# A two-block transformer kernel: the output product of the attention block in three split passes, its parts split between the heads, the pooling three heads earlier, the shift put into the rows by products

## The reference, cut to what matters

```
xl  = xl + g1 * (concat[a, b, p, h] @ w_out)      # a: differential attention, b: neighbourhood attention,
                                                  # p: pooling, h: long convolution; 256 features each
hl2 = rmsnorm(xl, norm2_g) * (1 + sc2) + sh2
gates = top-2 of softmax(hl2 @ router_w), inside the best group of 4 experts
for e in 16 experts:  out += gates[:, e] * ((silu(hl2 @ w1[e]) * (hl2 @ w3[e])) @ w2[e])
```

## Time and profile before

| | us |
|---|---|
| median of three runs | 1447.33 |
| the runs | 1447.38, 1447.33, 1444.16 |
| the profiled execution, device time | 1444.78 |
| its span, first to last instruction | 1442.9 |
| TensorE busy in the span | 1291.6 (90%) |
| DVE, ACT, POOL busy | 839.9, 569.7, 146.6 |
| mean granted TensorE clock | 0.936 of full speed |

### The profile page before, as it was taken

One profiled execution on the slowest core, in us unless ns is written; L12 is line 12 of the kernel. 1 busy time (PEld: TensorE's weight loads), 2 busy tenths in 40 slices (PEclk: granted clock), 3 DMA queues, 4 the chain that ended last, 5 costly groups with the idle time before them and its releaser, 6 DMA issues.

```text
span 1442.9 us, 16957 instructions
## 1 busy us (share of the span) xinstructions
PE 1291.6 (90%) x6470; PEld 929.9 (64%) x6470; DVE 839.9 (58%) x1238; ACT 569.7 (39%) x750; POOL 146.6 (10%) x130
## 2 busy tenths in 40 slices
PE   6999999987899898389999999769997899889796
PEld 2544466766768544268888888557875777775674
DVE  2347978636856204558888888546216457624453
ACT  1423001114544413057777777513324343334322
POOL 1100101000015002102222222020000000000000
PEclk9989999999999799599999999859999999889998
DMA  9523746564040020659999999833223654624301
GB/s 368 235 82 135 254 156 271 197 155 93 7 180 1 1 118 32 233 188 386 406 407 407 408 401 405 323 115 124 91 77 132 190 164 115 191 96 181 116 2 58
DMA packets 52838, 270.67 MB, mean 188 GB/s; under 512 B 15047, under 2 KB 22087, under 8 KB 38056
## 3 DMA queue, kind: packets, MB, share of 16 engines
q1 hardware_dynamic: 38280, 209.52, 39.4%
q0 software_dynamic: 9744, 47.19, 8.9%
q10 hardware_dynamic: 4752, 13.11, 2.3%
HBM read 229.42 MB, written 36.70 MB: 184 GB/s over the span
## 4 chain that ended last, share of the span: by engine, by line
PE 76%; DVE 11%; issue 4%; ACT 4%; DMA 4%; POOL 1%; SPq 0%; DVEq 0%; ACTq 0%; POOLq 0%
PE PS L2581 29%; PE PS L2965 7%; PE PS L2966 6%; PE PS L2967 6%; PE PS L3188 3%; PE PS L3189 3%; PE PS L3190 3%; PE PS L3094 2%; PE PS L3093 2%; PE PS L3095 2%; PE PS L2844 1%; PE PS L3174 1%; PE PS L2598 1%; PE PS L2959 1%; DMA ring<-in_slabs 1%
## 5 line engine op out<-in xcount | busy, mean ns | idle before, releaser
L2581 PE MATMUL PS<-arena 128*128 128x64 f32 (+7 forms) x786 | 196.2, 417 | 36.5 <-issue 9.8
L1305 ACT ACTIVATE arena_r<-ring 128x2048 fp32r<-128x2048 f32 x100 | 185.7, 1909 | 15.1 <-ACT arena L1334 9.4
L2581 PEld LDWEIGHTS PS<-arena 128*128 128x128 f32 (+2 forms) x786 | 122.0, 205 | 101.2 <-issue 78.4
L2581 PE MATMUL PS<-hT,ring 128*128 128x512 f32 (+1 forms) x432 | 176.8, 567 | 1.4 <-ACT hT L1287 1.4
L2054 DVE TENSOR_TENSOR arena_r<-ring,arena_r 128x2048 fp32r<-128x2048 f32 x66 | 148.2, 2287 | 10.4 <-ACT arena_r L1305 10.2
L2581 PEld LDWEIGHTS PS<-hT,ring 128*128 128x128 f32 x432 | 81.8, 192 | 93.4 <-issue 88.0
L3188 PE MATMUL PS<-arena_r 128*128 128x512 f32 x256 | 105.8, 413 | 16.6 <-DVE ring_r L2442 10.8
L2965 PE MATMUL PS<-arena_r,hT_r 128*128 128x512 f32 x272 | 112.8, 415 | 7.8 <-DVE arena_r L2054 5.4
L2966 PE MATMUL PS<-arena_r,hT_r 128*128 128x512 f32 x272 | 108.8, 400 | 0.0
L3190 PE MATMUL PS<-arena_r,ring_r 128*128 128x512 f32 x256 | 103.4, 404 | 0.0
L1158 ACT ACTIVATE arena<-PS 128x1024 f32<-128x1024 f32 (+3 forms) x32 | 29.1, 916 | 180.3 <-PE PS L2581 164.1
(11 more groups left out here) (421 smaller groups left out, 2321.5 us busy)
## 6 DMA issues: line engine op xcount, KB each, us to landing
ring<-in_moe SPq DMA_DIRECT2D x51, 2048.0 KB, 10.4
ring<-in_slabs SPq DMA_DIRECT2D x27, 2048.0 KB, 10.1
ring<-in_slabs SPq DMA_DIRECT2D x9, 1024.0 KB, 5.6
y_rows<-arena ACTq DMA_DIRECT2D x17, 512.0 KB, 10.0
ssm_scratch<-arena POOLq DMA_DIRECT2D x4, 1152.0 KB, 6.2
arena<-ssm_scratch POOLq DMA_DIRECT2D x4, 1152.0 KB, 9.0
arena<-in_tab_fwd SPq DMA_DIRECT2D x2, 2048.0 KB, 15.2
ssm_scratch<-arena POOLq DMA_DIRECT2D x4, 1024.0 KB, 10.5
```

Of the source, the lines that this page charges most:

```text
L1305: nc.scalar.activation(rounded(moe_w_hi[n][:, cols]), ring[:, n, cols], ACT.Copy).then_inc(s_moe_hi[n], 1)
L2581: ins = nc.tensor.matmul(out, lhsT, rhs, start=(n == 0), stop=(n == len(pairs) - 1))
```

## The change

Eight parts, each with its lines of the diff:

1. The four units "wo" are made in three passes on split operands. `mix_hi` holds the high parts of the eight row parts of `mixT`, `wo_hi` (three buffers in turn) the high part of a 128-column chunk of `w_out`; `mixT` and the slab themselves are overwritten with the low parts.
2. The splits of `mixT` are made between the heads of b: high parts by ACT, low parts by DVE. "ot", "ot_a" and "pm" are released by DVE instead of ACT.
3. "ot_a" moves from i = 8 to i = 12, two steps of the normalisation of a from heads 5 and 6 to 9 and 10, "pm" from behind the heads to i = 14, and POOL's start from the transposes of head 5 to those of head 2.
4. The square root is taken by ACT on the sums themselves, before they are transposed.
5. The shift enters each row through two products of 96 rows and 512 columns (`root_hi_lo`, `shift_hi_lo`), and POOL's addition is gone.
6. Row tile 3 is made behind "rank" instead of ahead of it.
7. W2 of tile 0 and W1, W3 of tile 1 are loaded only once the first gathered rows have landed, in the order W1, W2, W3. `moe_high(1, 0)` moves behind the row copies.
8. The split of W1 for tile 1 is made during tile 0.

```diff
-        if a == "b" and i == 8:
+        if a == "b" and i == 12:
             yield ("ot_a",)
...
+        if a == "b" and i == 14:
+            yield ("pm",)
...
-    u += [(("h_tr", t), "act") for t in range(QT)] + [(("rank",), "dve"), (("list",), "dve")]
+    u += [(("h_tr", t), "act") for t in range(QT - 1)] + [(("rank",), "dve"), (("h_tr", QT - 1), "act"), (("list",), "dve")]
...
             for t in range(QT):
-                sp.wait_ge(s_h_rows, t + 1)
+                read(sp, ("h_tr", t))
                 sp.dma_start(stream_rows[P * t:P * t + P], h_rows[:, t]).then_inc(s_rows, 16)
-            sp.dma_start(ring[:, 2], moe_d[2]).then_inc(s_moe_w[2], 16)
...
-            load_w1_w3(1)
+            sp.wait_ge(s_taken, 16)
+            e_1 = expert_of(1)
+            sp.dma_start(ring[:, 0], moe_d[bass.ds(3 * e_1, 1)]...)
+            sp.dma_start(ring[:, 2], moe_d[2]).then_inc(s_moe_w[2], 16)
+            sp.wait_ge(s_moe_lo[1], 2)
+            sp.dma_start(ring[:, 1], moe_d[bass.ds(3 * e_1 + 1, 1)]...)
...
-            filled(pool, ("b", "t", 5))
+            filled(pool, ("b", "t", 2))
...
-            for t in range(QT):
-                read(pool, ("h_tr", t))
-                nc.gpsimd.tensor_tensor(h_rows[:, t], h_rows[:, t], shift_rows, ALU.add).then_inc(s_h_rows, 1)
...
+            def wo_high(n):
+                slab_here(act, ("w_out", n // 4))
+                if n >= 3:
+                    wo_chunk_done(act, n - 3)
+                nc.scalar.activation(rounded(wo_hi[n % 3]), wo_weights(n), ACT.Copy).then_inc(s_w_a_hi, 1)
+            def during_b(i):
+                if 8 <= i < 10:
+                    act.wait_ge(s_gate, 4)
+                    nc.scalar.activation(rounded(mix_hi[:, i - 2]), mixT[:, i - 2], ACT.Copy).then_inc(s_op_hi, 1)
+                elif i == 13:
+                    act.wait_ge(s_pool_d, 4)
+                    wo_high(0)
...
+            wo_high(1)
+            wo_high(2)
             act.wait_ge(s_rt_w, 2)
...
-            copy_unit(("rs",), rt_sums[0:64], bank(("rs",), 0)[0:64])
-            root(4, rt_rstd)
+            nc.scalar.activation(rt_sums[32:64], bank(("rs",), 0)[32:64], ACT.Sqrt, scale=1.0 / D,
+                                 bias=eps_t[32:64]).then_inc(s_act_read, 1)
+            read(act, ("rs",))
+            for n in range(2):
+                nc.scalar.activation(rounded(root_hi_lo[32 * n:32 * n + 32]), rt_sums[32:64], ACT.Copy).then_inc(s_shift, 1)
...
+            moe_high(1, 0, False)
...
                 nc.scalar.activation(moe_s, PS[:, 0, :], ACT.Silu).then_inc(s_silu_m, 1)
+                if behind == 0:
+                    moe_high(0, j + 1)
...
+                if i in (8, 12, 13, 15, 16):
+                    mix_low({8: 1, 12: 4, 13: 5, 15: 6, 16: 7}[i])
                 output("b", i - 1)
...
+                if i in (11, 14):
+                    mix_low(2 if i == 11 else 3)
+            mix_low(8)
+            for n in range(3):
+                wo_low(n)
...
-                if j == 0:
-                    read(pe, ("pm",))
-                    pe.wait_ge(s_gate, 4)
...
                 for c in range(2):
-                    products(bank(key, c), [(w[:, k, col:col + P], mixT[:, k]) for k in range(KD)], last=(c == 1))
+                    n = 2 * j + c
+                    hi, lo = wo_hi[n % 3], wo_weights(n)
+                    order = (6, 7, 0, 1, 4, 5, 2, 3)
+                    passes = [[(hi, mix_hi, k) for k in order], [(hi, mixT, k) for k in order], [(lo, mix_hi, k) for k in order]]
+                    pe.wait_ge(s_w_a_hi, n + 1)
+                    for m, (w, x, k) in enumerate(sum(passes, [])):
+                        if n == 0 and m in (0, 4, 6):
+                            pe.wait_ge(s_op_hi, {0: 5, 4: 6, 6: 8}[m])
+                        if n == 0 and m == KD:
+                            pe.wait_ge(s_op_lo, 8)
+                        if m == 2 * KD:
+                            pe.wait_ge(s_w_a_lo, n + 1)
+                        ins = nc.tensor.matmul(bank(key, c), rounded(w[:, k]), rounded(x[:, k]), start=(m == 0), stop=(m == 3 * KD - 1))
...
+                for half in range(2):
+                    nc.tensor.matmul(bank(key, half), rounded(root_hi_lo[0:96, P * t:P * t + P]),
+                                     rounded(shift_hi_lo[0:96, 512 * half:512 * half + 512]), start=True, stop=False)
+                    for k in range(4 * half, 4 * half + 4):
...
+            pe.wait_ge(s_root_lo, 2)
-            for t in range(QT):
+            for t in range(QT - 1):
                 rows_of(t)
```

More of the change, by code:

```diff
@@ L119, in unit_of @@
     if kind == "ot_a":
-        return ("a", "ot"), "act"
+        return ("a", "ot"), "dve"
+    if kind == "pm":
+        return ("pm",), "dve"
     if kind == "s_b":
@@ L1294, in _ @@
                 ins.then_inc(s_diags, 1)
+            wo_high(3)
             copy_unit(("sr",), shift_rows, both(("sr",)))
+            read(act, ("sr",))
+            nc.scalar.activation(rounded(shift_hi_lo), shift_rows, ACT.Copy, scale=ada_sel[:, 0:1]).then_inc(s_shift, 1)
             copy_unit(("rc",), rt_const, bank(("rc",), 0)[:, 0:EXPERTS])
+            wo_high(4)
             def moe_high(n, j, again=True):
@@ L2220, in moe_tile @@
                                         as_float(taken_hi.rearrange(flat)), ALU.subtract).then_inc(s_taken_lo, 1)
+                if behind == 0:
+                    moe_low(0, j + 1)
+                if behind >= 2:
+                    moe_low(0, j)
                 if behind >= 1:
-                    moe_low(0, j)
                     moe_low(1, j)
@@ L2237, in _ @@
             moe_tile(0, 0)
-            with dve.Fori(1, tiles) as j:
-                moe_tile(j, 1)
+            moe_tile(1, 1)
+            with dve.Fori(2, tiles) as j:
+                moe_tile(j, 2)
             for c in range(2):
@@ L2863, in _ @@
                         ins.then_inc(s_filled, 1)
+                    elif turn[0] == "pm":
+                        start_unit(key)
+                        pe.wait_ge(s_pool_d, 4)
+                        for g in range(2):
+                            products(bank(key, g), [(pool_w[:, g], pool_d[:, g])], last=(g == 1))
                     else:
@@ L2867, in _ @@
                     out_tr(a, QT - 1)
-            key = ("pm",)
-            start_unit(key)
-            pe.wait_ge(s_pool_d, 4)
-            for g in range(2):
-                products(bank(key, g), [(pool_w[:, g], pool_d[:, g])], last=(g == 1))
             def w_out(j):
```

163 lines of the change are left out of this document (112 added, 51 removed).

## The result

The changed kernel took 1431.49 us, the median of four runs (1428.58 to 1432.74), beside 1445.86 us for the kernel before (four runs, 1444.16 to 1447.38): a ratio of 0.9898, 95% interval 0.9877 to 0.9919. It is faster by about 14 us, where 1416 and a range of 1407 to 1430 had been forecast. Measured again later, in five rounds beside other runs of before, it took 1427.44 us (nine runs, 1422.64 to 1434.30) against 1439.67, ratio 0.992, interval 0.9888 to 0.9953. The profiled execution took 1428.58 us with a span of 1426.8, which is 16.1 us under the span of before.

The account below looks back on a forecast made before the run. TensorE, with 76% of the chain, was taken as the bound. Terms 11.2 + 2.2 + 8.4 + 0.3 + 3.4 + 4.7 = 30.2 us off 1444.78 gave 1414.6, adjusted to 1416 us; range 1408 to 1424, with rivals 1407 to 1430.

Parts of the forecast that it names:

- The three passes: Output product: a unit of 48 split products takes 11.15 us instead of 13.95; 2.8 per unit, 11.2 us over four.
- Both lie beside PE: Output product: ACT's 1.06 and DVE's 1.23 us per chunk are covered by PE's 5.57; cost taken as 0.
- the old price: Output product: weight loads of changing stationary tiles set the pace, so 11.2 us is lost: 1427 us; chance 0.07.
- overlap: Output product: products sharing a stationary part run at half of 0.232 us, giving 1394 us; chance 0.01.
- a clock that stays down through the product: Output product: its products run at the lower clock, 37 us more, giving 1453 us; chance 0.05.
- The routing: Routing stretch: 8.4 us gained, 7.7 of it from dropping POOL's additions, plus 0.3 for "list".
- the clock falls in more places: Later heads and the wait of row tiles 0 to 2: up to 2 us per fall, 2 or 3 give 1421; chance 0.10.
- The end of the heads: Between the last transposes and the output product: 4.8 us leaves, 2.6 is exposed between the heads, net gain 2.2 us.
- Today 4.8 us pass: Kernel before, last transposes to first output product, 491.50 to 496.32: all 4.8 us was to leave.
- The gather: First gather: 8.09 us beside two 2 MB loads, fastest of its kind 4.2; holding loads back gains 3.4 us.
- Tiles 0 to 1: Wait for W1's split ahead of tile 1: 2.5 us of wait and 2.2 of clock gained, together 4.7 us.
- The rival on W3: W3 of tile 1 lands 17 to 21 us after the gather, ACT wants it at 19: 1422 us; chance 0.12.

Follow-up runs that it names:

- added products alone: The changed kernel with 24 extra products that nothing reads added on PE between the heads; 1414.99 us in one execution.
- pooling product last: The changed kernel with the pooling product and its two copies behind the last head again, parts 4 and 5 last in chunk 0; 1422.48 us in one execution.
- the kernel before with the added products: The kernel before with the same extra products, read by nothing, between its heads; 1435.82 us in one execution.
- the loads early: The changed kernel with each expert weight load sent as soon as its slot is free, none waiting for the gather; 1422.01 us in one execution.

## Why the prediction was right or wrong

**The three passes: right.** 2.8 us a unit were predicted. Units 1 to 3 take 11.24 and twice 11.38 us against 13.98, 2.6 to 2.7 less. Unit 0 took 12.7 us from its first product to what follows it (500.61 to 513.27) against 15.5 (496.32 to 511.82). "Both lie beside PE" held for all eight chunks. The rivals of the old price, of overlap and of a clock that stays down through the product all fell. The figure of 131 ns of the Trainium skill ("TensorE: Matmul & The Clock Gate", "Back-to-back issue gap") is not reached: a product took 11.38 / 48 = 0.237 us.

**The routing: right.** 8.7 us predicted, 8.3 found, and the experiment without POOL's additions gives the mechanism alone. That parts 4 to 6 would bring 1.0 net (0.7, and 0.3 for "list") was a sum of small terms; they brought 0.1. One loss is visible: PE waits 2.26 us before the row tiles, and the clock behind it is at 0.50 from 561.75 to 565.16, where before it was at 1.00 until 578. In the two traces with 25.6 us (added products alone, pooling product last) it stood there for 6.8 us instead of 3.4. The rival "the clock falls in more places" had named this place too.

**The end of the heads: wrong**, -2.2 predicted, +3.8 found, in three places.
- The step "DVE's low parts stand ahead of a scaling whose reader is a whole head away: 0" looked at the wrong reader. The low part itself releases a slot of PSUM, and PE waits for that. It was also placed wrongly in DVE's queue: the row maximum ahead of it waits for scores. At the upper clock this costs 1.9 us (63.3 - 61.4).
- "Today 4.8 us pass" was read at the lower clock, and from the end of the last transposes. From their start it is 496.32 - 490.85 = 5.5 us, and at the upper clock 489.49 - 485.96 = 3.5 us (the kernel before with the added products). In the changed kernel with the same products 0.2 are left of it. So the gain of moving the pooling product was 3.3 at best, and 1.1 by the experiment that undid it. PE's timeline of the kernel before, then of the kernel before with the added products, where these are read:

```profile
490.85 0.66 PE L2824 MATMUL PS<-ident,post 128*128 128x128 f32 x2 [0.54 <-DVE post L1985]
```
```profile
485.96 0.41 PE L2824 MATMUL PS<-ident,post 128*128 128x128 f32 x2 [0.54 <-DVE post L1985]
486.20 1.88 PE L2581 MATMUL PS<-arena 128*128 128x512 f32 x4
489.49 13.97 PE L2581 MATMUL PS<-hT,ring 128*128 128x512 f32 x32 [1.40 <-ACT hT L1287]
```

- The clock was not part of this term. It costs 3.3 us more than before in most executions, and 8.0 or 13.6 more where it falls early (75.8 or 81.4, less 63.3 and less the 4.5 of before). The rival "the clock falls in more places" named it, with 0.10 and up to 2 us a fall: the place was right, the chance and the size were too low. A wait of 1.46 us with a low clock behind it was on the table; the change adds waits, of 0.6 to 1.4 us, to stretches that ran at 1.00, and that alone should have raised the chance.

**The gather: a term mis-sized.** 3.4 predicted, 2.5 found. The 4.2 us of the earlier trace rows belonged to the second gather. The first one is a longer instruction on POOL, as its line shows in the changed kernel and the same line in the kernel before (ns min/median/max):

```profile
L1029 POOL DMA_INDIRECT arena<-stream_rows,arena x4: 961/976/2442, 581.9 to 622.1; - x4
```
```profile
L1009 POOL DMA_INDIRECT arena<-stream_rows,arena x3: 964/982/2440, 596.4 to 618.5; - x3
```

The 2.44 us are those of the first, and it lands in 5.5 us with no load under way. 4.2 + 1.46 = 5.7 was the price to take.

**Tiles 0 to 1: wrong**, -2.5 of wait predicted, +2.5 found. The step "with W1 split during tile 0 only the rows' own two parts stay" was right (2.43 us of wait found, 2.9 predicted). What failed is that the chain was followed only through tile 0's gather. The rival on W3 even said that "tile 1's own gather goes with them" and priced only W3. W3 landed some 20 us behind the first gather, within its 17 to 21, and PE did not wait for it. The gather took 12.4 us, PE stood 3.6, and the clock came down once more: 0.50 from about 603 to 606. Of the 5.9 us predicted for the two stretches ahead of tile 1's first product (3.4 and 2.5) nothing came (31.8 and 31.7 us); with the loads early 5.3 of them are there.

**The loop** was taken to keep its length, with the 2.2 us of clock gained at its start: right, 314.1 against 316.5. The windows are the first 8 us behind tile 1's first product, in the kernel before, in the changed kernel and with the loads early:

```profile
628.21:636.21 8.00, 8.00 (x27) 6.36 (x28) 6.46 (x3) 2.96 (x3) 0.00 (x0) 0.71 0.60 219
```
```profile
613.66:621.66 8.00, 8.00 (x41) 6.67 (x42) 5.19 (x3) 4.39 (x5) 0.18 (x1) 1.00 0.36 109
```
```profile
605.12:613.12 8.00, 8.00 (x31) 6.45 (x32) 4.50 (x2) 2.83 (x4) 0.00 (x0) 0.79 0.79 295
```

Means of 0.71 and 0.79 over 8 us are 4.6 and 3.4 us at 0.50. The four traces whose loop took 314.1 to 315.0 us have no lower clock in this place; the other ten, at 315.7 to 317.7, have 2.9 to 5.5 us of it, and half of that is what they are longer, within 0.9 us. In the changed kernel the clock had fallen earlier, from 603 to 606, behind the wait for the second gather. With the loads early that wait is gone, and the clock fell 0.9 us behind tile 1's first product instead: the 1.7 us given back are half of those 3.4.

## What to carry to other kernels

When an instruction moves to another engine's queue, ask which semaphore it feeds and who waits for that one, then put it ahead of whatever in that queue waits for something later. Work moved off a collision lands on the next transfer of the same kind: follow the chain to the second one. In a stretch whose clock has already fallen once, price a new wait of half a microsecond by the clock as well; a trace with harmless products filled in tells what the clock costs there. And book a gain of clock at the place where the lower clock stands, which can be a stretch later than the wait ahead of it.

## What was not expected of the hardware

- At the same idle of 0.63 us in the changed kernel's heads the clock came down in two executions of six and stayed at 1.00 in four. In one it then stood at 1.2 GHz (0.50) from 457 to 501 us, with PE busy 42.84 of the 43.00 us behind 458. The product units behind the heads ran at 1.00 in every trace after their first microseconds. The Trainium skill, page "TensorE: Matmul & The Clock Gate", has something on both sides. Its section "A second HAM failure mode: psum-queue depth-cycling" tells of frequent micro-idles between groups of products with which the clock goes up and down; the falls near waits of 0.6 to 1.5 us agree with that, and no run here tests the cycling through banks. The general rule in "What's actually happening", that activity releases the throttle, is not borne out by the 43 us at 0.50.
- 24 products that nobody reads made the kernel before 4.5 us and the changed kernel 7.8 us shorter in the heads.
- An indirect gather of 128 rows landed in 4.0 to 5.6 us with little beside it and in 11.5 to 12.4 behind three loads of 2 MB from another queue.
